# FFN weight sums on VectorE in place of GpSimd, with a new order on ScalarE, in a diffusion layer on one Trainium2 core

## The reference, cut to what matters

```python
def _conv_ffn(h, w_gu, conv_w, conv_b, w_down):
    g, u = jnp.split(h @ w_gu, 2, axis=-1)        # h: tokens x 1024, w_gu: 1024 x 5632
    ...
    for t in range(CONV_W):                       # width 3 along the tokens
        gc = gc + gp[:, t:t + L] * conv_w[t]
    return (jax.nn.silu(gc) * u) @ w_down
```

## Time and profile before

| | us |
|---|---|
| median of 3 runs | 3197.89 |
| lowest and highest run | 3193.79, 3198.98 |
| the profiled execution, own time | 3194.57 |
| its span, first to last instruction | 3192.8 |
| PE busy / PEld busy | 2902.6 / 2553.3 |
| DVE busy | 2005.9 |
| ACT busy | 1281.3 |
| POOL busy | 818.0 |

### The profile page before, as it was taken

How to read it: one execution, slowest core, us unless ns; L and a number is a source line. 1 busy time by engine, 2 the same in 40 slices (tenths; PEclk the granted TensorE clock), 3 DMA queues, 4 the chain that set the end, 5 groups by cost and what they waited for, 6 DMA issues and landing times. The chain is left out here.

```text
span 3192.8 us, 50797 instructions
## 1 busy us (share of the span) xinstructions
PE 2902.6 (91%) x17132; PEld 2553.3 (80%) x17132; DVE 2005.9 (63%) x3113; ACT 1281.3 (40%) x2746; POOL 818.0 (26%) x793
## 2 busy tenths in 40 slices
PE   4899999797999997998699988999899979999997
PEld 0799999545888886886699988998899978888875
DVE  3433432444989895677877788777877753543545
ACT  3111111114878885232455554554555542121121
POOL 0000000111322221222544445444444410302302
PEclk7999999898999998999799999999999989999999
DMA  7322221567346443454332323332233334333333
GB/s 244 98 83 91 84 89 63 207 210 196 86 105 139 99 95 94 150 183 140 98 91 90 95 86 118 100 93 89 78 95 101 90 113 145 117 125 113 117 118 135
DMA packets 358739, 372.29 MB, mean 117 GB/s; under 512 B 87686, under 2 KB 288789, under 8 KB 355893
## 3 DMA queue, kind: packets, MB, share of 16 engines
q1 hardware_dynamic: 339865, 360.86, 37.4%
q10 hardware_dynamic: 18720, 9.44, 1.0%
HBM read 271.10 MB, written 101.12 MB: 117 GB/s over the span
## 5 line engine op out<-in xcount | busy, mean ns | idle before, releaser
L1929 PE MATMUL fu_alpha<-fu_h,fu_w 128*128 128x384 f32 x3168 | 601.1, 342 | 82.7 <-ACT fu_u L2007 64.9
L1929 PEld LDWEIGHTS fu_alpha<-fu_h,fu_w 128*128 128x128 f32 x3168 | 561.2, 192 | 103.7 <-issue 45.4
L2390 PE MATMUL fd_acc<-fd_w,fd_f 128*128 128x512 f32 x2376 | 546.2, 392 | 26.0 <-DVE fd_w L2418 16.6
L2390 PEld LDWEIGHTS fd_acc<-fd_w,fd_f 128*128 128x128 f32 x2376 | 447.3, 189 | 124.8 <-issue 17.6
L1929 PE MATMUL fu_beta<-fu_h,fu_w 128*128 128x384 f32 x1584 | 287.3, 336 | 5.2 <-DVE fu_h L2130 5.2
L1929 PEld LDWEIGHTS fu_beta<-fu_h,fu_w 128*128 128x128 f32 x1584 | 277.3, 189 | 5.6 <-issue 5.6
L517 PE MATMUL pj_gps<-pj_ht,w_in 128*128 128x256 f32 x2160 | 268.1, 284 | 0.0
L2414 DVE TENSOR_TENSOR fd_f<-fd_f_stage,fd_f 128x512 fp32r<-128x512 f32 (+1 forms) x110 | 89.0, 810 | 284.3 <-ACT fd_f L2370 284.3
L517 PEld LDWEIGHTS pj_gps<-pj_ht,w_in 128*128 128x128 f32 x2160 | 262.7, 192 | 1.3
L2126 DVE TENSOR_TENSOR fu_w<-up_w_stage,fu_w 128x512 fp32r<-128x512 f32 x264 | 229.1, 869 | 43.9 <-ACT fu_w L1989 43.9
L2161 DVE SCALAR_TENSOR_TENSOR fu_result<-fu_g,fu_conv_w,fu_result 128x768 f32<-128x768 f32 (+1 forms) x132 | 212.1, 1607 | 61.7 <-ACT fu_result L2029 61.6
(11 more groups left out here) (199 smaller groups left out, 4794.8 us busy)
## 6 DMA issues: line engine op xcount, KB each, us to landing
up_w_stage<-in_w_gu_dram SPq DMA_DIRECT2D x132, 512.0 KB, 5.0
fd_w_stage<-in_w_down_dram SPq DMA_DIRECT2D x54, 512.0 KB, 3.6
fd_f_stage<-f_t SPq DMA_DIRECT2D x88, 256.0 KB, 2.7
at_k<-k_t SPq DMA_DIRECT2D x28, 704.0 KB, 12.7
fo_w<-in_w_ada_dram SPq DMA_DIRECT2D x8, 2048.0 KB, 8.7
ada_w_in_stage<-in_w_in_dram SPq DMA_DIRECT2D x48, 192.0 KB, 3.2
pj_x<-in_x_all_dram SPq DMA_DIRECT2D x9, 1024.0 KB, 4.9
mx_y<-y_mixed SPq DMA_DIRECT2D x18, 512.0 KB, 4.9
```

Source lines behind the costliest of these rows:

```text
L1929: mm = pe.matmul(out, w[x][:, j, k, :], b[y][:, j, k, :], start=opens and (k, x, y) == (0, HI, HI), stop=(k, x, y) == (KH - 1, LO, HI), sk ...
L2390: mm = pe.matmul(acc[:, t, at], f[a][:, slot, t * P:(t + 1) * P], w[b][:, w_at(st, slot), at], start=is_step(st, 0) and (a, b) == (HI, HI) ...
```

## The change

VectorE makes the four weight sums of every step (`first_weight_sums` three of them, `last_weight_sum` the fourth), with the code that GpSimd had. GpSimd keeps the hidden sums, cut into 16 slices of 128x384, one in each of steps 3 to 18, each released by `c11_done`; the two that are needed first (T3, T4 of the first span) it makes at once at the start. On ScalarE `copy_u3` of a step moves from the head of the next step to a place in its own step, behind the A12 rounding and ahead of the SiLU of the step before; on VectorE `add_c22` moves with it, to a place ahead of the gate. `ubuf` has two buffers.

```diff
-        ubuf = sb("fu_u", [P, SPAN])
+        ubuf = sb("fu_u", [P, 2, SPAN])
...
+                for q in (1, 2, 3):
+                    pool.wait_ge(up.h_staged[q], 16)
+                pool.wait_ge(t12_made, 4)
+                pool.tensor_tensor(up.hst[:, T3], up.hst[:, B22], up.hst[:, B12], ALU.subtract).then_inc(t34_made, 4)
+                pool.wait_ge(t12_made, 8)
+                pool.tensor_tensor(up.hst[:, T4], up.hst[:, B21], up.hst[:, T2], ALU.subtract).then_inc(t34_made, 4)
+
+                def hidden_sum(p, i, out, a, b, made_by):
+                    for k in range(KH):
+                        pool.wait_ge(c11_done, p * FT + 3 + i * KH + k)
+                        pool.tensor_tensor(up.hst[:, out, k], up.hst[:, a, k], up.hst[:, b, k], ALU.subtract).then_inc(made_by, 1)
+
+                for p in range(SPANS - 1):
+                    for q in range(4):
                         pool.wait_ge(up.h_staged[q], (p + 2) * 16)
+                    hidden_sum(p, 0, T1, B12, B11, t12_made)
...
 # ScalarE, step
-                    if before is not None:
-                        copy_u3(*before)
                     act.wait_ge(done[A11], n + 1)
...
                     if ends:
                         high_b(p + 1, A12)
+                    copy_u3(*now)
                     if before is not None:
                         silu(*before)
                         gate_edge(*before)
...
 # VectorE
+                def first_weight_sums(m, par):
+
+                    a = [[up.wst[:, par, h, kh * KH:(kh + 1) * KH, :] for kh in range(2)] for h in range(2)]
+                    dve.wait_ge(up.w_staged[par], (m - par) * 16 + 32)
+                    if from_step(m, 1):
+                        dve.wait_ge(w_lo, w_ready(m - 1, S1))
+                    dve.tensor_tensor(sums[:, 0], a[1][0], a[1][1], ALU.add).then_inc(made, 1)
+                    dve.wait_ge(made, m * 4 + 1)
+                    if from_step(m, 1):
+                        dve.wait_ge(w_lo, w_ready(m - 1, S2))
+                    dve.tensor_tensor(sums[:, 1], sums[:, 0], a[0][0], ALU.subtract).then_inc(made, 1)
+                    dve.tensor_tensor(a[1][0], a[0][0], a[1][0], ALU.subtract).then_inc(made, 1)
+
+                def last_weight_sum(m, par):
+                    dve.wait_ge(made, m * 4 + 2)
+                    if from_step(m, 1):
+                        dve.wait_ge(w_lo, w_ready(m - 1, S4))
+                    dve.tensor_tensor(sums[:, 2], up.wst[:, par, 0, KH:KT, :], sums[:, 1], ALU.subtract).then_inc(made, 1)
...
                 def add_c22(m, p, f, par):
                     dve.wait_ge(u3_done, m + 1)
-                    if from_step(m, 1):
-                        dve.wait_ge(u_kept, m)
-                        dve.wait_ge(gated, m)
-                    dve.tensor_tensor(ubuf[:, HALF:SPAN], beta[:, par, 0:HALF], u3[:, :], ALU.add).then_inc(c22_done, 1)
+                    if from_step(m, 2):
+                        dve.wait_ge(u_kept, m - 1)
+                        dve.wait_ge(gated, m - 1)
+                    dve.tensor_tensor(ubuf[:, par, HALF:SPAN], beta[:, par, 0:HALF], u3[:, :], ALU.add).then_inc(c22_done, 1)
...
 # VectorE, step
-                    if before is not None:
-                        add_c22(*before)
                     low_next(A11)
+                    if more:
+                        first_weight_sums(m, 1 - par)
                     low_now(A22)
                     low_next(S1)
                     if before is not None:
                         add_c12(*before)
                     low_now(S4)
+                    if more:
+                        last_weight_sum(m, 1 - par)
...
                     low_next(A12)
+                    add_c22(*now)
                     if before is not None:
                         gate(*before)
                     low_next(S3)
```

More of the change, by code:

```diff
@@ L1824, in ffn_up_phase, with after @@
         width = lambda p: SPAN if p < SPANS - 1 else SPAN + 2
+        def after(n, p, f, by=1):
+            if isinstance(f, int) and f + by >= FT:
+                return n + by, p + 1, f + by - FT
+            return n + by, p, f + by
         def w_source(m, par, j):
@@ L1857, in step @@
                     n, p, f, par = now
-                    if not isinstance(n, int) or n + 2 < STEPS:
+                    l, lp, lf = after(n, p, f, 2)
+                    if lp < SPANS:
                         sp.wait_ge(w_lo, w_count(n, A22))
                         sp.wait_ge(made, n * 4 + 4)
-                        up.load_w(sp, f + 2 if not isinstance(f, int) else (f + 2) % FT, par)
+                        up.load_w(sp, lf, par)
                     if fixed(f, 1) and p < SPANS - 1:
@@ L2010, in copy_c21 @@
                     act.wait_ge(done[A22], m + 1)
-                    if from_step(m, 1):
-                        act.wait_ge(gated, m)
-                    act.copy(ubuf[:, 0:HALF], alpha[:, par, 0:HALF]).then_inc(c21_done, 1)
+                    if from_step(m, 2):
+                        act.wait_ge(gated, m - 1)
+                    act.copy(ubuf[:, par, 0:HALF], alpha[:, par, 0:HALF]).then_inc(c21_done, 1)
                 par1 = lambda ap, f: ap[:, bass.ds(f, 1)]
@@ L2045, in gate_edge @@
                     act.wait_ge(zeroed, 4)
-                    act.copy(par1(u_edge[:, (p + 1) % 2], f), ubuf[:, SPAN - 1:SPAN]).then_inc(u_kept, 1)
+                    act.copy(par1(u_edge[:, (p + 1) % 2], f), ubuf[:, par, SPAN - 1:SPAN]).then_inc(u_kept, 1)
                     act.activation(res[:, par, 0:1], res[:, par, 0:1], ACT.Copy, scale=par1(u_edge[:, p % 2], f)).then_inc(edge_gated, 1)
@@ L2057, in step @@
                     more = not is_last(n)
+                    m, mp, _ = after(n, p, f)
                     ends = fixed(f, FT - 1) and p < SPANS - 1
                     begins = fixed(f, 0) and p > 0
-                    if before is not None:
-                        copy_u3(*before)
                     act.wait_ge(done[A11], n + 1)
@@ L2066, in step @@
                     if more:
-                        high_w(n + 1, 1 - par, A11)
+                        high_w(m, mp, 1 - par, A11)
                     if ends:
@@ L2071, in step @@
                         copy_c21(*before)
-                    high_w(n, par, A22)
+                    high_w(n, p, par, A22)
                     if begins:
@@ L2092, in step @@
                     if more:
-                        high_w(n + 1, 1 - par, A12)
+                        high_w(m, mp, 1 - par, A12)
                     if ends:
                         high_b(p + 1, A12)
+                    copy_u3(*now)
                     if before is not None:
@@ L2104, in end @@
                 def end(last):
-                    copy_u3(*last)
                     copy_c21(*last)
@@ L2111, in _ @@
                 for j in AT_ONCE:
[L2112 removed]
+                    high_w(0, 0, 0, j)
                     high_b(0, j)
@@ L2216, in end @@
                 def end(last):
-                    add_c22(*last)
                     add_c12(*last)
```

62 lines of the change are left out of this document (22 added, 40 removed).

## The result

The changed kernel takes 3119.89 us (median of 4 runs, 3115.98 to 3120.42) against 3195.84 us for the kernel before on the same chip (4 runs, 3193.69 to 3198.98): a ratio of 0.9759, 95% interval 0.9742 to 0.9776, some 76 us faster. The prediction said 3119. Its profiled execution took 3120.38 us, of which the span is 3118.6. Counted from ScalarE's first rounding of the phase to the end of the last S4's loads, the up half took 1076.63 us before and 1000.88 after: 75.75 less, while the whole spans differ by 74.2, so the gain lies in this phase.

The account below looks back on a forecast made before the run. TensorE was taken to bound the conv-FFN's up half, held up by waits; savings of 41 + 30.6 + 4.4 + 1 = 77.0 us from 3194.57 gave 3117.6, put at 3119 us, range 3104 to 3159.

Parts of the forecast that it names:

- The steady steps: TensorE's wait before A22 for the u3 copy goes: 0.73 us in each of 56 steps, 41 us saved.
- The sums on VectorE: Four weight sums add 2.76 us a step to VectorE, 2.75 is given back; its load stays at 11.68.
- The last rival: Nothing happens: added work equals that given back, SiLU passes its lateness to the next step; 3195 us, chance 0.03.
- The hidden sums: Slicing GpSimd's hidden sums removes four TensorE waits of 6.1 us and slow loads of 1.55 behind each: 30.6 us saved.
- The borders: At the two borders between token spans, waits with slower loads cost about 8 us against 10.2: 4.4 us saved in all.
- The lead-in: At the phase's start the first A11 comes 3.6 us later, S3 of step 1 about 1 earlier: 1 us saved.
- afterwards VectorE is met by less GpSimd work: Lead-in step, after the later first A11: S3 of step 1 starts about 1 us earlier.
- The sum: Steady steps, hidden sums, borders, lead-in: 41 + 30.6 + 4.4 + 1 = 77.0 us saved in the up half.
- GpSimd was to be under 60 us in the phase: Expected sign in the profile after: GpSimd's work in the conv-FFN's up half stays under 60 us.
- The wait at S3: Rival: VectorE over 1.9 us late at add_c12, TensorE waits for u2 instead; all 41 gone, 3159 us, chance 0.12.
- VectorE as the bound: Rival: VectorE's operations stay long, sums take 1.32 each, 16.95 us a step; slower, 3273 us, chance 0.05.

Follow-up runs that it names:

- run 1: Kernel before with only the new order (u3 copy and add_c22 moved, two ubuf buffers), GpSimd keeping all its sums whole: 3130.3 us, ratio 0.9788.
- run 2: Changed kernel with the old order back (copy_u3, add_c22 at the head of the next step), sums on VectorE and slices kept: 3123.14 us, ratio 0.977.
- run 4: Kernel before with the new order and sliced hidden sums, the weight sums left on GpSimd: 3116.57 us, ratio 0.9746.
- run 9: Changed kernel and run 4's kernel measured once more, unaltered, on one chip: 3121.9 us and 3114.83 us.
- run 3: Changed kernel with GpSimd's hidden sums whole again, two at step 2 and two at step 19 of a span: 3127.17 us, ratio 0.9779.
- Run 8: Run 4's kernel with the lead-in of run 7, GpSimd beginning with the weight sums of step 1: 3115.53 us, ratio 0.9745.
- Run 7: Changed kernel with another lead-in: VectorE makes T3, T4 of the first span, low A11 ahead of all sums: 3117.98 us, ratio 0.9752.
- run 6: Changed kernel with four more VectorE sums of 128x512 a step, results unused: 3138.14 us, ratio 0.9821.

## Why the prediction was right, and where it wasn't

**The steady steps, 41.** Right: 15.26 to 14.56 us a step, 56 x 0.70 = 39 us. The way was described rightly too (copy behind its product, VectorE first at `add_c12`), with 0.7 predicted and 0.68 measured before `add_c12`, 1.2 and 1.17 before S3. What the text didn't see is that this gain has two sufficient causes: the order without freed VectorE (run 1) and, in the old order, the sums on VectorE together with the slices (run 2) remove the same wait.

**The sums on VectorE, 0.** Right: 11.68 us a step predicted, 11.60 measured, each sum 0.69. Beside the new order and the slices the move brings nothing, and even cost 4.4 us (runs 4 and 9); in the old order, with the slices, it is enough for the steady steps (run 2). The Trainium skill says (Perfetto Trace Analysis, Optimizing Scalar/DVE Operations) that offloading work between these two engines might not help. Runs 4 and 9 are such a case; run 2 is one in which it helped, together with the slices. The last rival, no change at all, failed for the reason given there: in the list of waits after, TensorE never waits for SiLU or the gate.

**The hidden sums, 30.6.** Right in sum: all four waits and their slow loads are gone. The slices' share is smaller than the prediction has it, because the order alone already shrinks each of these waits from 6.1 to some 3 (run 1). From run 1 to run 4 the slices bring 13.7 us, in run 3 they are worth 7.3 (15.6 and 8.9 by the phase). A slice takes 1.38 us and not 1.06, a third and not a quarter of a whole sum; at its place it costs TensorE nothing, in run 4 not even at 1.74 among the weight sums.

**The borders, 8 each.** Near in size, 1.38 + 4.04 + 2.28 of slower loads = 7.7 and 1.38 + 4.05 + 1.53 = 7.0, against 10.2; so 5.7 us saved where 4.4 were predicted. That is luck in part, because two errors cancel: 2.2 and 4.8 at S3 and 0.3 for u3 were said, 7.3 of waiting where 5.4 were measured, and 0.7 for slower loads where they took 2.28 and 1.53. So the slower loads behind a wait are a term of their own, about a quarter of the price here. Run 4's border waits are 0.31, 1.98 and 2.63, 4.9 in all and near the 5.4 of after, but the clock stays at 1.00 behind the longest of them, and no load is slow. The length of that wait doesn't settle it: in run 1 the same wait is followed by loads at full pace at the first border and by slow ones at the second.

```profile
1893.32 6.20 PEld L1929 LDWEIGHTS fu_alpha<-fu_h,fu_w 128*128 128x128 f32 x36 [2.63 <-issue]
...
2225.51 7.76 PEld L1929 LDWEIGHTS fu_alpha<-fu_h,fu_w 128*128 128x128 f32 x36 [2.63 <-issue]
```

Behind the second the granted clock is down to 0.50 from 2227.50 to 2229.50. In runs 4, 8 and 9 none of the six waits of 2.60 to 2.63 had slow loads behind it; all waits of 3.79 us and more at the borders, in every run, had. The difference between the two kernels at the borders, 7.7 + 7.0 - 2 x 4.9 = 4.9 us, is 3.8 of slower loads and 1.1 of waiting. That it is the move which turns three waits into two longer ones was not tested by itself.

**The lead-in, 1.** Wrong by little: the first A11 came 2.9 us later (3.6 predicted), but S3 of step 1 0.3 later and not 1 earlier; in the changed kernel's second trace (run 9) it came 0.1 earlier. The step that failed is "afterwards VectorE is met by less GpSimd work": the two whole hidden sums still hold it for 3.80 and 3.95 us. Run 7 takes them away, puts low A11 first, and brings S3 2.9 us forward against the first trace, 2.5 against the second.

**The sum.** 39 + 30.6 + 5.7 - 0.3 = 75.0 against 77.0 predicted and 75.75 in the phase. That 3119 lies within 1 us of the median is luck: the steady steps and the lead-in brought 3.3 us less than said and the borders 1.3 more, 3119 was itself chosen between two starting points 3.3 apart, and the same kernel took 3121.9 in run 9. GpSimd was to be under 60 us in the phase; 32 slices at 1.38 and the two sums at the start make 52.

**The rivals.** The wait at S3 exists, but from 2.3 us of added VectorE work on (run 6), and the change adds none. VectorE as the bound would have needed sums of over 1.02; they took 0.69. In run 6, busy 189.25 of 200 us, VectorE came close to it.

## What to carry to other kernels

When one change has several parts, each may remove the same wait, so run each part alone before any is given the credit: here the order alone brought 66 us of 76 and the other half, the sums with the slices, 73; beside order and slices the part in the change's name cost 4. Before moving work between two engines that hold each other up, measure the slack ahead of the next product (here by adding operations until TensorE waits) and see whether the work lies inside it already. And where a wait can't be removed, read the granted clock behind it too: waits of 0.3, 2.0 and 2.6 us mostly cost less than waits of 1.4 and 4.0, behind the longer of which TensorE ran at half the clock each time.

## What the runs showed of the hardware

- VectorE and GpSimd hold each other up in both directions. The Trainium skill (SBUF — State Buffer, Who interferes with whom) has the shared pair as an exclusive lock for a whole instruction, and the rows of 3.80 to 4.26 us on VectorE beside GpSimd sums of 3.72 to 4.23 agree. Run 8 shows one GpSimd sum spread over 12.39 us while VectorE's operations follow each other without a gap: GpSimd came to its end only behind nine more of them. Of this a single row speaks, and spans on GpSimd are rough.
- VectorE's operations overlap when they stand back to back: a sum of 0.69 us occupies 0.60 from start to start, so the four of run 6 cost 2.41 and not 2.76.
- A cut instruction on GpSimd has its price: 128x1536 mostly takes 3.7 to 4.2 us beside a held VectorE, 128x384 1.38, so four slices take 5.5 us for the same work.
- After a wait of 4.04 us TensorE's granted clock read 0.50 for about 4 us, and 36 loads took 8.53 in place of 6.25 (7.76 to 7.78 behind the same wait at the second border and in run 9). After waits of 2.63 it read 1.00 in run 4 and at the first border of run 1, and fell to 0.50 at the second border of run 1. In run 3 it fell to 0.50 behind a wait of 2.13, and the 36 loads took 7.77.
